# Last layer's down projection with activations stationary and 512 weight columns moving, with its norm and store by tokens

## What is computed

```python
        h = rms_norm(r, norm_ffn_pre[layer])
        gu = h @ w_gate_up[layer].astype(dt)
        ff = (jax.nn.silu(gu[..., :D_FF]) * gu[..., D_FF:]) @ w_down[layer].astype(dt)
        r = r + rms_norm(ff, norm_ffn_post[layer])

    return r[:, N_META:N_META + s, :]
```

## Time and profile before

| what | value |
|---|---|
| median of 3 runs | 840.55 us (839.25 to 840.62) |
| the profiled execution, whole | 839.78 us |
| the profiled execution, span of the core | 837.8 us |
| mean granted TensorE clock, as a share of 2.4 GHz | 0.995 |
| PE busy / DVE busy / ACT busy / POOL busy, us of the span | 820.7 / 611.0 / 460.1 / 127.5 |
| last layer's down matmuls, first start to last start | 765.38 to 827.46 us |

### The profile page before, as it was taken

One profiled execution on the slowest core, in us unless ns is written; L12 is line 12 of the kernel. 1 busy time (PEld: TensorE's weight loads), 2 busy tenths in 40 slices (PEclk: granted clock), 3 DMA queues, 4 the chain that ended last, 5 costly groups with the idle time before them and its releaser, 6 DMA issues.

```text
span 837.8 us, 17756 instructions
## 1 busy us (share of the span) xinstructions
PE 820.7 (98%) x6711; PEld 805.3 (96%) x6711; DVE 611.0 (73%) x1015; ACT 460.1 (55%) x754; POOL 127.5 (15%) x131
## 2 busy tenths in 40 slices
PE   8999999999999999999999999999999999999995
PEld 8998999999999999999999999899999999999995
DVE  5899586569597666666668995866787877667763
ACT  6656555474565444455556556555665744545550
POOL 2112000004331111101112220000143111111010
PEclk9999999999999999999999999999999999999998
DMA  8666423225536555356653665233462665644631
GB/s 289 217 186 203 146 77 101 80 98 190 163 101 217 184 158 186 116 153 183 188 173 107 196 200 178 76 102 101 147 208 75 224 197 182 193 145 150 192 124 51
DMA packets 40554, 131.05 MB, mean 156 GB/s; under 512 B 4528, under 2 KB 5936, under 8 KB 40496
## 3 DMA queue, kind: packets, MB, share of 16 engines
q1 hardware_dynamic: 40496, 130.24, 48.8%
HBM read 129.18 MB, written 1.05 MB: 155 GB/s over the span
## 4 chain that ended last, share of the span: by engine, by line
PE 80%; DVE 14%; ACT 2%; issue 2%; DMA 1%; POOL 0%; SPq 0%; DVEq 0%; POOLq 0%
PE bank L1059 23%; PE bank L1061 22%; PE bank L1060 22%; DVE w_lo L660 4%; PE bank L1089 2%; PE bank L1284 2%; PE bank L1260 2%; PE bank L1108 1%; DVE h_lo L682 1%; PE bank L1299 1%; PE bank L1093 1%; DVE resid L697 1%; DVE tres L690 1%; DVE lat_lo L781 1%; ACT e_t L450 1%
## 5 line engine op out<-in xcount | busy, mean ns | idle before, releaser
L660 DVE TENSOR_TENSOR w_lo<-w_raw,w_hi 128x1024 fp32r<-128x1024 f32 x260 | 347.8, 1344 | 21.7 <-ACT w_hi L321 19.5
L1059 PE MATMUL bank<-h_hi,w_hi 128*128 128x272 f32 (+1 forms) x1232 | 358.3, 291 | 1.9 <-DVE lat L678 0.7
L1061 PE MATMUL bank<-h_hi,w_lo 128*128 128x272 f32 (+1 forms) x1232 | 352.8, 286 | 0.0
L1060 PE MATMUL bank<-h_lo,w_hi 128*128 128x272 f32 (+1 forms) x1232 | 351.8, 286 | 0.0
L321 ACT ACTIVATE w_hi<-w_raw 128x1024 fp32r<-128x1024 f32 x260 | 273.0, 1054 | 117.4 <-PE bank L1061 67.8
L1059 PEld LDWEIGHTS bank<-h_hi,w_hi 128*128 128x128 f32 x1232 | 232.6, 189 | 4.1 <-issue 2.2
L1061 PEld LDWEIGHTS bank<-h_hi,w_lo 128*128 128x128 f32 x1232 | 232.4, 189 | 0.0
L1060 PEld LDWEIGHTS bank<-h_lo,w_hi 128*128 128x128 f32 x1232 | 232.2, 188 | 0.0
L1061 PE MATMUL bank<-ff_hi,w_lo 128*128 128x272 f32 (+1 forms) x352 | 100.0, 284 | 0.0
L1059 PE MATMUL bank<-ff_hi,w_hi 128*128 128x272 f32 (+1 forms) x352 | 99.9, 284 | 0.0
L1060 PE MATMUL bank<-ff_lo,w_hi 128*128 128x272 f32 (+1 forms) x352 | 99.7, 283 | 0.0
(11 more groups left out here) (195 smaller groups left out, 1101.0 us busy)
## 6 DMA issues: line engine op xcount, KB each, us to landing
w_raw<-weights SPq DMA_DIRECT2D x198, 512.0 KB, 3.8
w_raw<-weights SPq DMA_DIRECT2D x32, 384.0 KB, 3.1
w_raw<-weights SPq DMA_DIRECT2D x32, 320.0 KB, 2.8
resid<-x_t SPq DMA_DIRECT2D x4, 272.0 KB, 4.7
out_t<-resid SPq DMA_DIRECT2D x4, 256.0 KB, 2.1
cst<-consts SPq DMA_DIRECT2D x1, 544.0 KB, 5.7
y<-consts SPq DMA_DIRECT2D x1, 256.0 KB, 4.9
b_t<-lam SPq DMA_DIRECT2D x1, 256.0 KB, 5.7
```

What stands on the lines that cost most here:

```text
L660: dve.tensor_tensor(w_lo[:, n % RING, :], w_raw[:, n % RAW, :], w_hi[:, n % RING, :].bitcast(f32), ALU.subtract).then_inc(lo_ready, 1)
L1059: pe.matmul(dst, wh, hi, start=first, stop=False)
L1060: pe.matmul(dst, wh, lo, start=False, stop=False)
L1061: return pe.matmul(dst, wl, hi, start=False, stop=last)
```

## The change

The last layer's down projection is turned round, and with it all that follows. Layer 0 keeps the old form.

- **Transposes of the residual stream.** After the last gate/up tile PE transposes the 16 blocks of 128x128 of `r` (8 channel chunks by 2 chunks of 128 tokens) into banks 4 to 7, and ACT copies them to `r_tok`, tokens on the partitions, in four copies of 512 columns between its splits.
- **Matmuls.** A slot now holds one inner chunk of all 1024 output channels, so the stage has 22 slots of 128x1024 in place of 32 of 768 or 640 columns. The stationary operand is a 128x128 block of `ff_hi` or `ff_lo` (128 inner channels by 128 tokens), the moving one 512 columns of `w_hi` or `w_lo`. Banks 0 to 3 hold the products of the two token chunks (c) by the two halves of channels (n). The first 14 slots are used for all four banks at once (12 matmuls a slot). The last eight (`TAIL`) stay in the ring of eight: first both halves of token chunk 0, then the first half of chunk 1 over the eight slots, then its second half. Before the first, PE waits until all gate/up tiles have left their banks (`tile_free`).
- **Norm.** A token is a partition now. ACT squares a bank of 512 columns and sums it along the row in the same step (`accum_out`); the second half's root takes the first half's sum as its bias (`o_bias`, made by DVE). DVE multiplies the bank by the gain row (`gain_bc`, a new load of 512 KB behind the last weights), takes the reciprocal of the root, and makes the product with it plus `r_tok` in one instruction for each half.
- **Store.** Four stores of 128x512 (256 KB) to an output that is laid out by tokens.
- POOL does nothing in this stage, and PE no sums and no spreading.

```diff
+
+def ends_of(l, name):
+
+    return [1] * (FC - TAIL) + [0] * TAIL if name == "down" and l == DEPTH - 1 else ENDS[name]
 
...
@@ -288,22 +306,27 @@
             first = 6
             for l in range(DEPTH):
                 d0 = plan.slot[l, "down", 0]
-                whole = (d0 - first) // RING
+                end = d0 if l < DEPTH - 1 else plan.slots
+                whole = (end - first) // RING
                 with sp.Fori(0, whole) as i:
                     for j in range(RING):
                         load(first + j, SLOT, i, RING)
-                for n in range(first + whole * RING, d0):
+                for n in range(first + whole * RING, end):
                     load(n, SLOT)
-                with sp.Fori(0, KC // 2) as i:
-                    for j in range(RING):
-                        load(d0 + j, DOWN_SPLIT[j % 4] * P, i, RING)
-                first = d0 + 4 * KC
-
-            out = outT.rearrange("p (k t) -> p k t", k=KC)
-            for c in range(0, KC, 2):
-                sp.wait_ge(r_ready, KC * (2 * DEPTH - 1) + c // 2 + 1)
-                sp.dma_start(out[:, c:c + 2, :], r[:, c:c + 2, N_META:TOK]).then_inc(out_done, 16)
-            sp.wait_ge(out_done, 16 * KC // 2)
+                if l < DEPTH - 1:
+                    with sp.Fori(0, KC // 2) as i:
+                        for j in range(RING):
+                            load(d0 + j, DOWN_SPLIT[j % 4] * P, i, RING)
+                    first = d0 + 4 * KC
+
+            sp.wait_ge(pe_done, plan.tile_done[plan.tile[DEPTH - 1, "out", KC - 1]])
+            sp.dma_start(gain_bc[:, :], gain_rows).then_inc(gain_rows_in, 16)
+            for c in range(2):
+                for n in range(2):
+                    cols = slice(n * HALF, (n + 1) * HALF)
+                    sp.wait_ge(o_ready, 2 * c + n + 1)
+                    sp.dma_start(out[c * P:(c + 1) * P, cols], o_tok[:, c, cols]).then_inc(out_done, 16)
+            sp.wait_ge(out_done, 16 * 4)
 
...
-
-                for m in range(KC):
-                    for j in range(4):
-                        split(SD + 4 * m + j + HI_AHEAD)
-                    square_tile(K0 + POST_FFN, TD + m, m)
-                root(K0 + POST_FFN, 7, D_MODEL, t0)
                 if l < DEPTH - 1:
+                    for m in range(KC):
+                        for j in range(4):
+                            split(SD + 4 * m + j + HI_AHEAD)
+                        square_tile(K0 + POST_FFN, TD + m, m)
+                    root(K0 + POST_FFN, 7, D_MODEL, t0)
                     boundary(2 * l + 2, K0 + NORMS + PRE_MIX, G_MIXPRE, l + 1)
+
+            split(SD + HI_AHEAD)
+            act.wait_ge(r_turned, 1)
+            for q in range(4):
+                c, n = q // 2, q % 2
+                act.activation(r_tok[:, c, n * HALF:(n + 1) * HALF], ps[4 + q][:, :], ACT.Copy).then_inc(r_tok_ready, 1)
+                split(SD + 1 + q + HI_AHEAD)
+            for k in range(5, FC):
+                split(SD + k + HI_AHEAD)
+            act.activation(idle_act, eps, ACT.Sqrt)
+            for c in range(2):
+                for n in range(2):
+                    act.wait_ge(o_done, 2 * c + n + 1)
+                    act.activation(o_sq[:, c, n * HALF:(n + 1) * HALF], ps[2 * c + n][:, :], ACT.Square,
+                                   accum_out=o_sum[:, 2 * c + n:2 * c + n + 1]).then_inc(o_summed, 1)
+                act.wait_ge(o_summed, 2 * c + 2)
+                act.wait_ge(o_biased, c + 1)
+                act.activation(o_std[:, c:c + 1], o_sum[:, 2 * c + 1:2 * c + 2], ACT.Sqrt, bias=o_bias[:, c:c + 1], scale=1.0 / D_MODEL).then_inc(o_rooted, 1)
...
@@ -633,8 +673,8 @@
                 with pool.Fori(0, 5) as i:
                     for j in range(2, 6):
                         product(j, i)
-                sum_squares(K0 + POST_FFN, t0)
                 if l < DEPTH - 1:
+                    sum_squares(K0 + POST_FFN, t0)
                     sum_squares(K0 + NORMS + PRE_MIX, 0)
...
-                for m in range(KC):
-                    for j in range(4):
-                        split(S("down") + 4 * m + j + AHEAD)
-                    to_y(K0 + POST_FFN, TL("down") + m, m)
...
                 if l < DEPTH - 1:
+                    for m in range(KC):
+                        for j in range(4):
+                            split(S("down") + 4 * m + j + AHEAD)
+                        to_y(K0 + POST_FFN, TL("down") + m, m)
+                    recip(K0 + POST_FFN, t0)
+                    dve.wait_ge(norm_bc, K0 + POST_FFN + 1)
                     residual(2 * l + 2, K0 + POST_FFN, G_FFNPOST, l, t0)
 
-            rstd2 = ps[7][:, None, 64 + N_META:64 + TOK].to_broadcast([P, 2, SEQ])
-            for c in range(0, KC, 2):
-                after(step(dve.tensor_tensor(y[:, c:c + 2, N_META:], y[:, c:c + 2, N_META:], rstd2, ALU.mult)))
-                dve.tensor_tensor(r[:, c:c + 2, N_META:], r[:, c:c + 2, N_META:], y[:, c:c + 2, N_META:], ALU.add).then_inc(r_ready, 1)
+            for k in range(FC):
+                split(S("down") + k + AHEAD)
+            dve.wait_ge(gain_rows_in, 16)
+            dve.wait_ge(r_tok_ready, 4)
+            for c in range(2):
+                halves = [slice(n * HALF, (n + 1) * HALF) for n in range(2)]
+                for n, cols in enumerate(halves):
+
+                    dve.wait_ge(o_summed, 2 * c + n + 1)
+                    if n == 0:
+                        dve.tensor_scalar(o_bias[:, c:c + 1], o_sum[:, 2 * c:2 * c + 1], 1.0 / D_MODEL, EPS, ALU.mult, ALU.add).then_inc(o_biased, 1)
+                    dve.tensor_tensor(o_tok[:, c, cols], ps[2 * c + n][:, :], gain_bc[:, cols], ALU.mult).then_inc(o_scaled, 1)
+                dve.wait_ge(o_rooted, c + 1)
+                dve.reciprocal(o_rec[:, c:c + 1], o_std[:, c:c + 1]).then_inc(o_inverse, 1)
+                dve.wait_ge(o_inverse, c + 1)
+                dve.wait_ge(o_scaled, 2 * c + 2)
+                for cols in halves:
+                    dve.scalar_tensor_tensor(out=o_tok[:, c, cols], in0=o_tok[:, c, cols], scalar=o_rec[:, c:c + 1], in1=r_tok[:, c, cols],
+                                             op0=ALU.mult, op1=ALU.add).then_inc(o_ready, 1)
...
+                if l == DEPTH - 1:
+                    continue
...
+
+            for q in range(4):
+                a, f0 = N_META + P * (q // 2), 4 * (q % 2)
+                for f in range(4):
+                    mm = pe.transpose(ps[4 + q][:, f * P:(f + 1) * P], r[:, f0 + f, a:a + P], ident)
+            mm.then_inc(r_turned, 1)
+
+            d0, g_last = S("down"), TL("gu") + 2 * FC
+
+            def part(k, c, n):
+
+                at, n0 = N_META + P * c, (d0 + k) % RING
+                x_hi, x_lo = ff_hi[:, k, at:at + P], ff_lo[:, k, at:at + P]
+                wh, wl = (w[:, n0, n * HALF:(n + 1) * HALF] for w in (w_hi, w_lo))
+                dst = ps[2 * c + n][:, :]
+                pe.matmul(dst, x_hi, wh, start=k == 0, stop=False)
+                pe.matmul(dst, x_hi, wl, start=False, stop=False)
+                return pe.matmul(dst, x_lo, wh, start=False, stop=k == FC - 1)
+
+            pe.wait_ge(tile_free, g_last)
+            for k in range(FC - TAIL):
+                slot_ready(d0 + k)
+                pe.wait_ge(ff_lo_ready, FC * (DEPTH - 1) + k + 1)
+                for c in range(2):
+                    for n in range(2):
+                        mm = part(k, c, n)
+                mm.then_inc(pe_done, 1)
+            for k in range(FC - TAIL, FC):
+                slot_ready(d0 + k)
+                pe.wait_ge(ff_lo_ready, FC * (DEPTH - 1) + k + 1)
+                for n in range(2):
+                    mm = part(k, 0, n)
+                    if k == FC - 1:
+                        mm.then_inc(o_done, 1)
+            for n in range(2):
+                for k in range(FC - TAIL, FC):
+                    mm = part(k, 1, n)
+                mm.then_inc(o_done, 1)
 
...
+        if l == DEPTH - 1:
+            for k in range(FC):
+                put(S("down") + k, [blocks(w_down[l], k, k + 1, 0, D_MODEL)])
+            continue
...
```

47 lines of the change are left out of this document (24 added, 23 removed).

## The result

The changed kernel takes **835.38 us** (median of 4 runs, 835.16 to 835.84), the kernel before, timed beside it, 840.36 us (4 runs, 839.25 to 840.62). The ratio is 0.9949, 95% interval 0.9936 to 0.9961: faster by 4.3 us, 3.3 to 5.4. The forecast was 837.9 with a range of 835.2 to 839.8, so the time lies inside it and on the side forecast, but only 0.2 us above its low end.

The account below looks back on a forecast made before the run. PE, busy without a gap in the down stage, was taken to bound the kernel, followed by a tail where it hardly works. -0.7 + 1.8 - 4.5 + 0.7 = -2.7 us from 840.55 gave 837.9 us, range 835.2 to 839.8.

Parts of the forecast that it names:

- Matmuls: Last layer's down stage: 264 matmuls of 512 columns at 232.8 ns replace 528 of 256 at 117.8 ns; -0.7 us.
- Rival (c): Down matmuls give nothing (235.6 ns) and the two last stores go one after the other; -1.4, 839.2 us; chance 0.13.
- (a): Down matmuls: the 11.1 ns beyond the columns are fixed, 224.4 ns at 512 columns; -5.0, 835.6 us; chance 0.14.
- (b): Down matmuls run at full rate at 512 columns, 215 ns, like plain fp32; -7.4, 833.1 us; chance 0.09.
- rival (d): Down stage slower: ACT and DVE write the weight ring that PE now reads as moving operand; 846.1 us; chance 0.07.
- Transposes: Before the down matmuls: 16 new fp32 transposes on PE, 1.73 us, plus 0.08 for a slow first matmul; +1.8 us.
- Supply of weights: Down stage: fewer splits gain nothing, and no weight slot or gain load comes late; put at nothing.
- Tail: After E, when the last matmul has taken in its columns: last DVE instruction ends E + 3.16, against 7.65; -4.5 us.
- Store: End of the span: last store waits 0.67 us for the one before, at 5.2 ns a KB; +0.7 us.

Follow-up runs that it names:

- e1: Changed kernel with each down matmul of 512 columns cut into two of 256, activations still stationary; 836.12 us, ratio 0.9957.
- e3: Changed kernel with the last eight slots used for all four banks together, so both token chunks finish at the end; 837.38 us, ratio 0.9968.
- e4: Changed kernel with the 16 transposes of the residual stream done twice; 837.51 us, ratio 0.9973.
- e5: Changed kernel with twelve of the 16 transposes moved forward among the last layer's first gate/up matmuls; 835.26 us, ratio 0.9949.
- e9: Changed kernel with TAIL, the number of last slots kept for the split end, cut from 8 to 4; 835.43 us, ratio 0.9951.
- e6: Changed kernel with one store of 512 KB for each token chunk in place of two of 256 KB; 836.25 us, ratio 0.9963.
- e0: The changed kernel without any edit, timed again beside later experiments; 836.16 us, ratio 0.9953.

## Why the prediction was right, and where it was off

**Matmuls.** Forecast 232.8 ns and -0.7 us; measured 231.7 and -0.95 (with the first, slow one in it). The split of the cost by three rows held: 0.449 ns a column, as forecast; the fixed part is 1.6 ns, not the 2.8 that I took from bf16, and e1 shows that it is an average over slots that differ by 6 ns. Rival (c) wanted 235.6, (a) 224.4, (b) 215, and all three fall by the spacing of the starts. By the rule of the Trainium skill named in the prediction (TensorE: Matmul & The Clock Gate, section Back-to-back issue gap) it would have been 215.8; the trace disagrees. The page gives the rule for a single matmul on its own, and for a stream at 512 columns some 131 ns, from which these fp32r matmuls are further still. But e1 shows that only some 0.4 us come from the length of the matmuls: 0.6 come with the new form of the stage at equal length of the matmuls, which I had put at nothing, and which stays unexplained. (0.4 and 0.6 are from starts alone; the slow first matmul takes some of it back.) Two errors are in this term, 0.3 too much for the length and 0.6 too little for the rest; that they partly cancel is luck.

**Contention, rival (d).** It fell altogether: PE's pace is 231.7 ns while ACT and DVE split, and there is no gap. Behind the last split it is 230.9 against 232.0 earlier, half a per cent. Even that isn't owed to the splits: in e1 the pace is slower behind the last split (117.2 against 116.4), and in e3, with the old order of the last slots, it stays at 231.8 against 232.0.

**Transposes.** Forecast +1.8 (1.73 and 0.08); measured 1.66 and 0.09. This is the difference to the kernel before, and e4 confirms the price of one more. Not all of the 1.66 is the transposes' own: e5 shows that PE would wait for the last gate/up bank anyhow, so that the first down matmul comes at least 0.80 us behind the last gate/up one, 0.68 more than before. The prediction had put this wait at 0.6.

**Supply of weights.** Forecast at nothing. PE is busy in all 63.00 us of the stage, and e9, which makes PE stay longer on four of the slots, changes nothing. The gain load took 6.7 us to land beside the weights, not 3.8, and was still far from late.

**Tail.** Forecast E + 3.16, measured E + 3.14. Step by step: square at E + 0.20 as forecast; product at E + 0.92 against 0.94 (0.90 and DVE's 0.04); reciprocal over at E + 1.68 against 1.72; the pair takes 1.42 against 0.74 + 0.66 = 1.40. Rows of nearby shapes were enough for each, and the waits between engines came out right because they were read at the same places before.

**Store.** This is the term that was mis-sized: forecast +0.7, measured -0.1. I had 5.2 ns for a KB, worked out from the difference of two load sizes in their time to landing. For these stores it is 2.3 (one more KB, e6) to 3.0. By the packet records the last store's data start 0.70 us behind those of the store before it, and the two were issued 0.66 us apart: the last waits 0.04 us, where I had 0.67. The step that failed is the use of loads for a store at the end of the span. That their landing includes what else was on its way is only a part of it: a load of 320 KB in the kernel before whose data flow alone (issued at 747.54) takes 1.37 us from its first packet to its last, 4.3 ns a KB. Why loads flow more slowly than stores, no run tells. The -0.1 fits the packet records: the last store of before went out in 1024-byte packets (0.89 us of data), after's in 2048-byte ones (0.81).

**The sum.** -0.95 + 1.66 - 4.51 - 0.11 = -3.91 by the traces, where I had -2.7. Of the 1.2 us between, 0.8 are the store, 0.25 the matmuls and 0.15 the transposes. The ratio says -4.3 (3.3 to 5.4). The median of 835.38 is another 1.3 us below what the traces give (840.55 - 3.91 = 836.6). The difference is as large as the scatter ahead of the stage, and e0's median stands 0.8 higher. It needs no cause in the change, and none is shown.

The time came out beside rival (a)'s 835.6, yet (a) is refuted: its pace of 224.4 ns is not there. Had I looked at the time alone, I would have learned the wrong mechanism.

**Open.** Why fp32r matmuls of 256 columns are 1.15 ns faster on average in the new form of the stage; why their cost moves by 6 ns with a period of four slots; why an fp32r column takes 0.449 ns, where one column a cycle at 2.4 GHz would be 0.417.

## What to carry to other kernels

At the end of a kernel count what still has to run behind the last matmul, and of what. Here eight elementwise instructions were most of it. A layout in which the norm's factor is one number per partition lets one instruction apply it and add the residual: 2.6 us. Finishing the banks one by one gave 1.4, the sum along an engine's own row in place of PE's sums and spreading 0.5, and matmuls of twice the length 0.4. Work added to an engine without gaps costs its full price (16 more transposes, 1.75 us), unless it goes where the engine waits; and what it hides itself has to be counted before it is moved (e5). For the last store take a rate from the flow of packets, not from a difference of landing times, and compare a stretch of the trace that repeats (to 0.01 us here) where the time of the whole scatters by one.
